# Hymba block with hierarchical MoE on one core: first weight group, gate weights and zero fills issued behind the first barrier

## The chip, the cores and the metric

One core of a Trainium2 chip runs the whole program in one launch. The metric is the device time of that core in microseconds (us). Engines are named as in the profile: PE is TensorE (matmul), PEld its weight loads, DVE is VectorE, ACT is ScalarE, POOL is GpSimd, SP is SyncE, which here only issues DMAs. A name with q behind it (SPq, POOLq, PEq) is that engine's sequencer.

## What is computed

A residual block over 4096 tokens (plus 16 meta tokens) of width 1024, then a sparse mixture of experts.

```
h = concat([meta, x])
h = h + hybrid_mixer(rmsnorm(h, mix_norm), w_in, ..., w_out)
h = h + hierarchical_moe(rmsnorm(h, ffn_norm), group_w, expert_w, w_gate, w_up, w_down)
out = rmsnorm(h, final_norm)[:, 16:]

def hybrid_mixer(u, ...):
    xb, gb, q, k, v, z, b_logit, a_logit = split(u @ w_in)     # w_in: 1024 x 3080
    y_lru = rmsnorm(rglru(xb, gb; w_r, w_i are 8 blocks of 64x64), g1)
    y_dn  = gated_deltanet(q, k, v, z, b_logit, a_logit)
    return concat([y_lru, y_dn]) @ w_out                       # w_out: 1024 x 1024
def hierarchical_moe(u, ...):
    # top-1 of 4 groups, top-2 of its 8 experts, blocks of tokens sorted by expert,
    # h = silu(x w_gate) * (x w_up);  y = h w_down;  scatter-add with the gate
```

## The kernel before

The program has four parts, each a block of five instruction streams (one for each engine) with barriers of all engines between them: an opening block (lines 320 to 410), the mixer and router (lines 478 to 1684), the experts, and the final norm. Behind the opening block stands `retire(...)` (line 412): a barrier, the clearing of semaphores by SP, and a second barrier.

In the opening block SP issues the DMAs of the first 128 tokens (`x_in`), of the router's columns (`gw`, which lies in `yl`), of the first of six groups of columns of `w_in` (`load_group(sp, "xb")`, 512 columns, 2048 KB), and, once POOL has zeroed two tiles, the four DMAs that put the blocks of `w_r` and `w_i` on the diagonals of `wr_bd` and `wi_bd`. ACT issues eight DMAs of small columns and then works out three of them, DVE zeroes state and finishes what ACT began, and POOL zeroes tiles, issues six DMAs (the last 128 rows of `u_rows` and `h_rows` in HBM from the zeroed tile `ht`, 512 KB each, and four fills of the table `idx_tab` from `qkT`, 256 KB each) and builds constants.

In the mixer's block SP issues the other five groups in the order q, k, v, gb, z, then `w_out` (4096 KB), then the second tile of x, then chunks of the experts' weights (`raw_chunks`, line 485) into `ht`, the first of which waits until the fills of the opening have landed. Each stream then runs steps i = -2, -1, 0, ... The steps -2 and -1 prepare the weights:

- DVE at i = -2: `router_columns` (L1231 to L1216), then `scale_of(0)`: L1186 takes the largest magnitude in the group xb, L1168 to L1172 with PE find it over all partitions, L1189 to L1192 make scales.
- DVE at i = -1, for each group g: `scale_of(g + 1)`, then `low_halves(g)` (L1200, eight of them). ACT makes the high halves (L887), POOL copies them into place (`high_copied`, L1692).
- The semaphore of the groups q and k is one, so `scale_of(1)` waits until both have landed.
- PE at i = -1, for g = 0 to 3: `largest` (L531, L533), `project` of group g (L578), then `router_turn` of two blocks of `w_out` (L543) and `router_through` (L553). `router_turn(0)` is the first that waits for `w_out`.
- POOL at i = -2: `level_masks` (L1706 to L1719).

From step 0 on a loop over 33 tiles of 128 tokens follows, in which PE is busy nearly all the time.

Of the kernel before, what the change touches and what calls it, by code (L numbers as in the profile page):

```python
# [21 lines left out]
P = 128  # L22
D = 1024
SEQ = 4096
# [18 lines left out]
IDX_FILLS = 2 * NE * TCAP // P // 512  # L43
# [16 lines left out]
I32 = mybir.dt.int32  # L60
# [4 lines left out]
GROUPS = ["xb", "q", "k", "v", "gb", "z"]  # L65
# [56 lines left out]
def hymba_block(nc, xm, w_in, w_out, conv_w, lru_cols, w_r, w_i, mix_g, ffn_g, final_g, dn_g, dn_a,  # L122
                dn_dt, w_router, b_router, w_gate, w_up, w_down, out):
    with ExitStack() as ctx:
        def sb(name, shape, dt=F32):
            return ctx.enter_context(nc.sbuf_tensor(name, shape, dt))
# [3 lines left out]
        def sem(name):  # L130

            if name not in sems:
                sems[name] = nc.alloc_semaphore(name=name)
            return sems[name]
# [25 lines left out]
        h_rows = nc.dram_tensor("h_rows", [SEQ + P, D], F32, kind="Internal").ap()  # L160
        u_rows = nc.dram_tensor("u_rows", [SEQ + P, D], F32, kind="Internal").ap()
        idx_tab = nc.dram_tensor("idx_tab", [NE * TCAP, 2], I32, kind="Internal").ap()
# [14 lines left out]
        wr_bd = sb("wr_bd", [P, 4, P])  # L177
        wi_bd = sb("wi_bd", [P, 4, P])
# [71 lines left out]
        qkT = sb("qkT", [P, 4, P])  # L250
# [24 lines left out]
        ht = sb("ht", [P, D])  # L275
# [38 lines left out]
        def load_group(sp, g):  # L314

            c, wide = COL[g], 512 if g != "z" else PROJ - COL["z"]
            sp.dma_start(wi[:, :, c:c + wide], w_in.rearrange("(p k) n -> p k n", k=KT)[:, :, c:c + wide]
                         ).then_inc(sem(LOADED[g][0]), 16)

        with nc.Block() as block:  # L320
            @block.sync
            def _(sp):

                sp.dma_start(x_in[:], xm[0:P, :]).then_inc(sem("x_in"), 16)
                sp.dma_start(gw, w_router.rearrange("(p k) n -> p k n", k=KT)).then_inc(sem("w_rt_in"), 16)
                load_group(sp, "xb")
                sp.wait_ge(sem("blocks_zero"), 1)

                for dst, src in ((wr_bd, w_r), (wi_bd, w_i)):
                    pair = src.rearrange("(j b) c d -> b c j d", b=2)  # L330
                    for b in range(2):
                        sp.dma_start(dst[64 * b:64 * b + 64, :, 64 * b:64 * b + 64], pair[b]).then_inc(sem("bd_in"), 16)

            @block.scalar
            def _(act):
# [41 lines left out]
            @block.gpsimd  # L377
            def _(pool):
                nc.gpsimd.memset(wr_bd[:], 0.0)
                nc.gpsimd.memset(wi_bd[:], 0.0).then_inc(sem("blocks_zero"), 1)  # L380
                nc.gpsimd.iota(io_i[:], pattern=[[1, NE]], base=0, channel_multiplier=0).then_inc(sem("iota_i"), 1)
                nc.gpsimd.iota(ip_i[:], pattern=[[0, 1]], base=0, channel_multiplier=1).then_inc(sem("iota_i"), 1)

                fill = qkT[:].rearrange("p a b -> p (a b)").bitcast(I32)
                nc.gpsimd.memset(ht[:], 0.0)
                nc.gpsimd.memset(fill, 0).then_inc(sem("zero_i"), 1)
                pool.wait_ge(sem("zero_i"), 1)
                nc.gpsimd.iota(fill.rearrange("p (m n c) -> p m n c", n=P, c=2)[:, :, :, 0], pattern=[[0, 2], [1, P]], base=SEQ,
                               channel_multiplier=0).then_inc(sem("zero_i"), 1)
                nc.gpsimd.memset(ones[:], 1.0).then_inc(sem("p_const"), 1)  # L390
                pool.wait_ge(sem("zero_i"), 2)
                for rest in (u_rows, h_rows):
                    pool.dma_start(rest[SEQ:SEQ + P, :], ht[:]).then_inc(sem("idx_zeroed"), 16)
                for n in range(IDX_FILLS):
                    pool.dma_start(idx_tab.rearrange("(p n) o -> p (n o)", p=P)[:, 512 * n:512 * n + 512],
                                   fill).then_inc(sem("idx_zeroed"), 16)
                pool.wait_ge(sem("p_const"), 1)

                nc.gpsimd.affine_select(out=ident[:], in_=ones[:], compare_op=ALU.is_equal, fill=0.0, base=0,
                                        pattern=[[1, P]], channel_multiplier=-1).then_inc(sem("p_const"), 1)  # L400
                nc.gpsimd.affine_select(out=tri[:], in_=ones[:], compare_op=ALU.is_ge, fill=0.0, base=0,
                                        pattern=[[1, P]], channel_multiplier=-1).then_inc(sem("p_const"), 1)
                nc.gpsimd.affine_select(out=kd[:, 3, :], in_=ones[:], compare_op=ALU.is_gt, fill=0.0, base=0,
                                        pattern=[[1, P]], channel_multiplier=-1).then_inc(sem("p_const"), 1)


                pool.wait_ge(sem("p_const"), 4)
                nc.gpsimd.tensor_copy(tri16[:], kd[:, 3, :]).then_inc(sem("p_const"), 1)
                nc.gpsimd.tensor_copy(ones16[:], ones[:]).then_inc(sem("p_const"), 1)
                pool.wait_ge(sem("p_const"), 6)  # L410
# [12 lines left out]
        def flat(t):  # L423
            return t[:].rearrange("p a b -> p (a b)")
# [53 lines left out]
        with nc.Block() as block:  # L478
            @block.sync
            def _(sp):  # L480
                for g in GROUPS[1:]:
                    load_group(sp, g)
                sp.dma_start(wo, w_out.rearrange("(k p) n -> p k n", p=P)).then_inc(sem("w_out_in"), 16)

                def raw_chunks(s):

                    if isinstance(s.i, int) and s.i == -1:
                        sp.wait_ge(sem("idx_zeroed"), ZEROED)
                    for n in s.sums:
                        for c in range(KT):  # L490
                            if c > 1 or n:
                                need(sp, sem("w_sq"), s.squares + KT * n + c - 1)
                            src = (w_gate, w_up)[c // 4][bass.ds(s.first + n, 1)].rearrange("o (p k) f -> p (o k f)", k=KT)
                            sp.dma_start(ht[:, 512 * (c % 2):512 * (c % 2) + 512], src[:, 512 * (c % 4):512 * (c % 4) + 512]
                                         ).then_inc(sem(f"w_raw{c % 2}"), 16)
# [1191 lines left out]
            def _(pool):  # L1687
# [36 lines left out]
                def o_copied(s, pieces):  # L1724

                    if isinstance(s.i, int) and s.i in pieces:
                        for n in range(*pieces[s.i]):
                            k, half = divmod(n, 2)
                            pool.wait_ge(sem("o_low"), n + 1)
                            nc.gpsimd.tensor_copy(wo16[:, k, w_half(True, 512 * half, 512)], o_room(n)).then_inc(sem("o_split"), 1)  # L1730

                def body(s):
                    if s.i == -2:
                        level_masks()
                    if s.i == -1:
                        for g in range(len(GROUPS)):
                            high_copied(g)
# [20 lines left out]
                    if s.G:  # L1758
                        need(pool, sem("ib_step"), 2 * s.nG)
                        need(pool, sem("gx_ready"), s.nG)  # L1760
                        b = nc.gpsimd.tensor_tensor(gx[:], gx[:], hh, ALU.mult)
                        if isinstance(s.i, int) and s.i == 0:
# [3 lines left out]
                            b = nc.gpsimd.memset(gx[:, :, 0:PAD], 0.0)  # L1766
# [415 lines left out]
```

## Time and profile before

| | |
|---|---|
| median of 3 runs | 3272.18 us |
| lowest, highest | 3269.68, 3272.93 us |
| the profiled execution's own time | 3265.26 us |
| its span, first to last instruction | 3263.7 us |
| busy: PE, DVE, ACT, POOL | 2990.4, 2590.6, 1997.9, 949.3 us |
| DMA bytes, mean rate | 380.30 MB, 117 GB/s |

The times of the views are counted from the start of the span. A row of the timeline reads: start, time taken (of all in the row), engine, line, operation, tile written <- tiles read, count, and in brackets how long the engine was idle before it and what ended that. SP's DMA rows give the time of issuing; the time to landing (the semaphore's last step) stands in the DMA views.

### The profile page before, as it was taken

The numbers are of one execution on the slowest core, as the hardware profiler recorded it, in microseconds if no ns is written. First come the engines' busy times: TensorE is split into PE (matmuls) and PEld (weight loads), VectorE is DVE, ScalarE is ACT, GpSimd is POOL, SyncE is SP. The second block draws the span as 40 slices with busy tenths as digits, with TensorE's granted clock in tenths as the row PEclk, the third lists the DMA queues.
The fourth block names the chain that finished last, engine by engine and source line by source line (L and its number), as shares of the span: only waits on it lengthen the run. The fifth ranks groups of instructions, "written<-read, shape, count | busy, mean of one in ns | idle before, by whom it ended". The sixth has DMA issues, their size and how long they took to land. (4 is left out here: it accounts for less than half of the span.)

```text
span 3263.7 us, 81939 instructions
## 1 busy us (share of the span) xinstructions
PE 2990.4 (92%) x28778; PEld 2233.3 (68%) x28779; DVE 2590.6 (79%) x7206; ACT 1997.9 (61%) x4412; POOL 949.3 (29%) x994
## 2 busy tenths in 40 slices
PE   3777999999999999999999999997699999999970
PEld 3766878888887888788878888885344555555430
DVE  6878778887887888788878887886788888888755
ACT  4555566666665656565666666653577777777646
POOL 4313122212221222132222212221344444544420
PEclk9889999999999999999999999998899999999985
DMA  7010111211212111212111111214387877677749
GB/s 264 27 53 14 47 66 65 67 66 66 72 63 76 60 67 66 73 60 73 66 66 65 68 66 66 72 56 200 118 255 222 243 202 214 187 219 216 220 99 394
DMA packets 117811, 380.30 MB, mean 117 GB/s; under 512 B 18560, under 2 KB 18688, under 8 KB 105216
## 3 DMA queue, kind: packets, MB, share of 16 engines
q1 hardware_dynamic: 82528, 269.96, 22.6%
q0 software_dynamic: 29216, 89.30, 11.9%
q10 hardware_dynamic: 5760, 16.85, 1.3%
q8 instruction: 204, 3.34, 0.4%
q14 instruction: 103, 0.84, 0.1%
HBM read 280.05 MB, written 96.01 MB: 115 GB/s over the span
## 5 line engine op out<-in xcount | busy, mean ns | idle before, releaser
L578 PE MATMUL pj<-uT,W 128*128 128x128 f16 x15840 | 982.9, 220 | 0.0
L578 PEld LDWEIGHTS pj<-uT,W 128*128 128x128 f16 x15840 | 936.8, 98 | 45.7 <-issue 37.6
L2038 DVE SCALAR_TENSOR_TENSOR W<-W,ecol 128x512 f16<-128x512 f16 x664 | 447.6, 747 | 111.9 <-ACT W L1982 107.4
L1982 ACT ACTIVATE W<-W,ecol 128x512 f16 x664 | 416.2, 710 | 79.7 <-issue 77.2
L1946 PE MATMUL bA<-W,uT 128*128 128x512 f16 x1992 | 446.6, 381 | 5.4 <-issue 4.1
L1946 PEld LDWEIGHTS bA<-W,uT 128*128 128x128 f16 x1992 | 193.5, 98 | 228.6 <-issue 9.1
L1741 POOL TENSOR_TENSOR dec<-tri,g 128x512 f32<-128x512 f32 x33 | 34.4, 1042 | 925.6 <-DVE g L1461 925.6
L1930 PE MATMUL pj<-W,qs 128*128 x664 | 301.8, 598 | 1.9 <-issue 1.0
L917 ACT ACTIVATE ht<-ht 128x512 f32<-128x512 f32 x256 | 159.9, 627 | 94.6 <-DMA ht<-w_up 90.2
L1930 PEld LDWEIGHTS pj<-W,qs 128*128 128x128 f32 x664 | 120.9, 192 | 123.3 <-issue 122.9
L947 ACT ACTIVATE qh<-bA 128x256 f32<-128x256 f32 x198 | 76.8, 388 | 193.4 <-PE bA L678 188.1
L638 PE MATMUL bO<-W,yl 128*128 128x512 f16 x768 | 186.4, 383 | 5.0 <-DVE yl L1375 5.0
L595 PE MATMUL pj<-W,uT 128*128 128x512 f16 x792 | 186.7, 379 | 0.5 <-POOL W L1692 0.5
L1777 POOL TENSOR_TENSOR yg<-aahh,gg 128x512 f32<-128x512 f32 x33 | 41.9, 1271 | 482.1 <-DVE yl L1375 457.8
L638 PE MATMUL bO<-W,yt 128*128 128x512 f16 x768 | 178.4, 378 | 0.0
L1155 DVE SCALAR_TENSOR_TENSOR qs<-ext_q,cvw,qs 128x128 f32<-128x128 f32 x396 | 168.2, 485 | 1.2
L678 PE MATMUL bA<-dec,Mt 128*128 128x128 f32 x792 | 134.2, 292 | 11.5 <-DVE dec L1303 11.1
L1906 POOL DMA_INDIRECT h_rows<-lath,sid x42 | 71.7, 1706 | 245.0 <-issue 121.1
L1906 POOL DMA_INDIRECT h_rows<-aahh,sid x41 | 71.0, 1731 | 203.6 <-issue 99.8
L595 PEld LDWEIGHTS pj<-W,uT 128*128 128x128 f16 x792 | 73.9, 98 | 71.7 <-issue 0.7
L1313 DVE COPY_PREDICATED X<-lvl,bB 128x256 f32<-128x256 uint8 x165 | 82.3, 499 | 50.5 <-PE bB L691 47.6
L691 PE MATMUL bB<-X,qh 128*128 128x128 f32 x660 | 113.4, 295 | 6.7 <-ACT qh L947 3.2
(444 smaller groups left out, 6310.0 us busy)
## 6 DMA issues: line engine op xcount, KB each, us to landing
ht<-w_gate SPq DMA_DIRECT2D x128, 256.0 KB, 3.2
ht<-w_up SPq DMA_DIRECT2D x128, 256.0 KB, 3.4
W<-w_gate SPq DMA_DIRECT2D x32, 1024.0 KB
W<-w_up SPq DMA_DIRECT2D x32, 1024.0 KB
W<-w_down SPq DMA_DIRECT2D x32, 1024.0 KB
x_in<-xm SPq DMA_DIRECT2D x33, 512.0 KB, 4.5
ht<-xm SPq DMA_DIRECT2D x32, 512.0 KB, 3.5
h_rows<-ht SPq DMA_DIRECT2D x32, 512.0 KB
```

Of the source, the lines that this page charges most:

```text
L578: mm = pe.matmul(pj[g % 2][:, j, :], w16[:, k, w_half(w_high, COL[GROUPS[g]], 512, j * P, P)], (ul if low_u else uh)[:, k, :], start=(k == ...
L595: mm = pe.matmul(flat(pj[1]), u[:, k, :], w16[:, k, w_half(w_high, c, 512)], start=(k == 0 and n_pass == 0), stop=(k == KT - 1 and n_pass ...
L638: mm = pe.matmul(bOf[:, 512 * half:512 * half + 512], y, wo16[:, j, w_half(w_high, 512 * half, 512)], start=(j == 0 and not w_high), stop= ...
L678: mm = pe.matmul(bA[:, q, :], Mt[:, 2 + q, :], crossed(T, b, P * q, HALF // b), start=True, stop=True)
L691: mm = pe.matmul(bB[:, q, :], Y[:, q, :], crossed(X, b, P * q, HALF // b), start=True, stop=True)
L917: nc.scalar.activation(ht[:, 512 * (c % 2):512 * (c % 2) + 512], ht[:, 512 * (c % 2):512 * (c % 2) + 512], ACT.Square, accum_out=sqc[:, n, ...
L1155: a = nc.vector.scalar_tensor_tensor(out=dst[:, j, :], in0=src, scalar=w, in1=dst[:, j, :], op0=ALU.mult, op1=ALU.add)
L1906: pool.indirect_dma_start(out=h_rows, out_offset=bass.IndirectOffsetOnAxis(ap=sid[par][:], axis=0), in_=yo[par], in_offset=None, compute_o ...
L1930: mm = pe.matmul(flat(pj[half]), hm2[:, j, :], w[:, j, 512 * half:512 * half + 512], start=(j == 0), stop=(j == 1))
L1946: mm = pe.matmul(flat(bA), x[:, k, :], wx[par][:, part, k, :], start=(k == 0 and part == 0 and x is uh), stop=(k == KT - 1 and x is ul))
L1982: nc.scalar.activation(part_of(wx[par][:, 0], k), raw[:, k], ACT.Copy, scale=ecol[par][:, k:k + 1]).then_inc(sem("wx_high"), 1)
L2038: a = nc.vector.scalar_tensor_tensor(out=part_of(wx[par][:, 1], k), in0=raw[:, k], scalar=ecol[par][:, k:k + 1], in1=part_of(wx[par][:, 0] ...
```

## The change

SP's opening stream keeps only the DMAs of `x_in` and the router columns. The group xb becomes the first of six in the mixer's block, and the four DMAs of `w_r` and `w_i` stand behind `w_out`, without the wait for POOL's zeroing, which the barrier now covers. POOL's six DMAs leave the opening block and stand in the mixer's block behind `level_masks`, ahead of the first `high_copied`.

```diff
             def _(sp):
                 sp.dma_start(x_in[:], xm[0:P, :]).then_inc(sem("x_in"), 16)
                 sp.dma_start(gw, w_router.rearrange("(p k) n -> p k n", k=KT)).then_inc(sem("w_rt_in"), 16)
-                load_group(sp, "xb")
-                sp.wait_ge(sem("blocks_zero"), 1)
-
-                for dst, src in ((wr_bd, w_r), (wi_bd, w_i)):
-                    pair = src.rearrange("(j b) c d -> b c j d", b=2)
-                    for b in range(2):
-                        sp.dma_start(dst[64 * b:64 * b + 64, :, 64 * b:64 * b + 64], pair[b]).then_inc(sem("bd_in"), 16)
...
                 pool.wait_ge(sem("zero_i"), 2)
-                for rest in (u_rows, h_rows):
-                    pool.dma_start(rest[SEQ:SEQ + P, :], ht[:]).then_inc(sem("idx_zeroed"), 16)
-                for n in range(IDX_FILLS):
-                    pool.dma_start(idx_tab.rearrange("(p n) o -> p (n o)", p=P)[:, 512 * n:512 * n + 512],
-                                   fill).then_inc(sem("idx_zeroed"), 16)
                 pool.wait_ge(sem("p_const"), 1)
...
-                for g in GROUPS[1:]:
+                for g in GROUPS:
                     load_group(sp, g)
                 sp.dma_start(wo, w_out.rearrange("(k p) n -> p k n", p=P)).then_inc(sem("w_out_in"), 16)
+                for dst, src in ((wr_bd, w_r), (wi_bd, w_i)):
+                    pair = src.rearrange("(j b) c d -> b c j d", b=2)
+                    for b in range(2):
+                        sp.dma_start(dst[64 * b:64 * b + 64, :, 64 * b:64 * b + 64], pair[b]).then_inc(sem("bd_in"), 16)
...
+                def table_filled():
+
+                    fill = flat(qkT).bitcast(I32)
+                    for rest in (u_rows, h_rows):
+                        pool.dma_start(rest[SEQ:SEQ + P, :], ht[:]).then_inc(sem("idx_zeroed"), 16)
+                    for n in range(IDX_FILLS):
+                        pool.dma_start(idx_tab.rearrange("(p n) o -> p (n o)", p=P)[:, 512 * n:512 * n + 512],
+                                       fill).then_inc(sem("idx_zeroed"), 16)
+
                 def body(s):
                     if s.i == -2:
                         level_masks()
+                        table_filled()
```

What stands on SP before, from the start of the opening block to the first chunks of expert weights (`yl` is the tile that holds the router columns, L153 the clearing of semaphores between the two barriers):

```order
2 L324 DMA x_in<-xm 128x1024
3 L325 DMA yl<-w_router 128x288
4 L317 DMA W<-w_in 128x8x512
5 L332 DMA wr_bd<-w_r 64x4x64 x2
6 L332 DMA wi_bd<-w_i 64x4x64 x2
7 L320 UNCONDITIONAL_BRANCH
8 L153 ISA x2
9 L479 UNCONDITIONAL_BRANCH
10 L317 DMA W<-w_in 128x8x512 x4
11 L317 DMA W<-w_in 128x8x520
12 L483 DMA W<-w_out 128x8x1024
13 L500 DMA x_in<-xm 128x1024
```

And with the change:

```order
2 L324 DMA x_in<-xm 128x1024
3 L325 DMA yl<-w_router 128x288
4 L320 UNCONDITIONAL_BRANCH
5 L153 ISA x2
6 L467 UNCONDITIONAL_BRANCH
7 L317 DMA W<-w_in 128x8x512 x5
8 L317 DMA W<-w_in 128x8x520
9 L471 DMA W<-w_out 128x8x1024
10 L475 DMA wr_bd<-w_r 64x4x64 x2
11 L475 DMA wi_bd<-w_i 64x4x64 x2
12 L492 DMA x_in<-xm 128x1024
13 L486 DMA ht<-w_gate 128x512 x4
```

The fifth 2048 KB load of `w_in` now stands in the same row of six as the others, all behind the barrier, and the small blocks stand between `w_out` and the second tile of x.

On POOL, the end of the opening block before:

```order
14 L390 MEMSET ones 128x128
15 L393 DMA u_rows<-ht 128x1024
16 L393 DMA h_rows<-ht 128x1024
17 L395 DMA idx_tab<-qkT 128x512 x4
18 L399 AFFINE_SELECT ident<-ones 128x128
19 L401 AFFINE_SELECT tri<-ones 128x128
20 L403 AFFINE_SELECT kd<-ones 128x128
```

And with the change, the place behind the masks in the mixer's block:

```order
47 L1728 DMA h_rows<-ht 128x1024
48 L1730 DMA idx_tab<-qkT 128x512 x4
49 L1684 COPY W<-rnq 128x512
50 L1684 COPY W<-decb 128x512
51 L1684 COPY W<-qh 128x512
```

The six fills (the one of `u_rows` stands in the row ahead of these) now come between the last mask and the first copy of a high half.

## Rows read from the trace of the kernel before

**Rows 1.** The page: span, and busy time of PE.

```profile
span 3263.7 us, 81939 instructions
...
PE 2990.4 (92%) x28778; PEld 2233.3 (68%) x28779; DVE 2590.6 (79%) x7206; ACT 1997.9 (61%) x4412; POOL 949.3 (29%) x994
```

**Rows 2.** Waits in 0 to 60 us (total, times, longest), then SP's queue.

```profile
POOL Mt L1706 <- POOLq L154: 9.5, 1, 9.5
...
SPq L320 <- PEq L320: 6.8, 1, 6.8
```

**Rows 3.** Timeline of the opening block and the barrier.

```profile
1.89 0.66 SPq L317 DMA_DIRECT2D W<-w_in  x1
...
3.34 0.76 ACTq L339 DMA_DIRECT2D dnc<-dn_g  x1
...
4.33 0.75 POOL L393 DMA_DIRECT2D u_rows<-ht  x1 [0.18 <-issue]
...
9.67 0.15 DVE L374 CAST tokf<-ip_i 128x1 f32<-128x1 int32 x1
...
18.69 16.57 SPq L317 DMA_DIRECT2D W<-w_in  x5
```

**Rows 4.** The four idx_tab fills: issue time, starts, time to landing.

```profile
L395 POOL DMA_DIRECT2D idx_tab<-qkT x4: 542/544/547, 5.6 to 7.2; - x4
...
DMA to landing us min/median/max: 9.0/9.7/10.2
```

**Rows 5.** Issues, KB each, us to landing: before 18.6 us, then at 18.69.

```profile
W<-w_in SPq DMA_DIRECT2D x1, 2048.0 KB, 15.7
...
dnc<-dn_g ACTq DMA_DIRECT2D x1, 0.5 KB, 9.1
...
W<-w_in SPq DMA_DIRECT2D x1, 2048.0 KB, 9.2
```

**Rows 6.** Timeline of DVE behind the barrier.

```profile
18.73 0.73 DVE L1231 TENSOR_TENSOR yl<-yl,fg 128x288 f32<-128x288 f32 x1 [8.92 <-PEq L154]
...
23.77 4.42 DVE L1186 TENSOR_REDUCE wmx<-W 128x8 f32<-128x4096 f32 x1
...
32.37 0.21 DVE L1445 TENSOR_SCALAR rxc<-xst,rdsc 128x1 f32<-128x1 f32 x1
33.02 4.42 DVE L1186 TENSOR_REDUCE wmx<-W 128x8 f32<-128x4096 f32 x1 [0.45 <-DMA W<-w_in]
```

**Rows 7.** Timeline where w_out is first used.

```profile
59.73 0.53 PEld L543 LDWEIGHTS bA<-ident,W 128*128 128x128 f32 x4 [0.17 <-DMA W<-w_out]
...
66.04 0.28 DVE L1170 TENSOR_REDUCE wm<-bO 1x1 f32<-1x128 f32 x1 [2.60 <-PE bO L531]
```

**Rows 8.** Busy time by stretch; last: PEclk, DMA share, GB/s.

```profile
18.00:20.50 2.50, 0.37 (x1) 0.08 (x1) 1.26 (x3) 1.79 (x2) 1.64 (x3) 1.00 0.11 12
...
24.00:32.00 8.00, 2.05 (x9) 1.27 (x7) 6.62 (x11) 1.93 (x4) 6.60 (x20) 1.00 1.05 399
```

**Rows 9.** Timeline of POOL: first mask, last mask, first copy.

```profile
18.71 0.72 POOL L1706 TENSOR_SCALAR_AFFINE_SELECT Mt<-ones 128x128 f32<-128x128 f32 x1 [9.52 <-POOLq L154]
...
31.16 0.53 POOL L1719 CAST lvl<-ot 128x128 uint8<-128x128 f32 x2
46.09 0.62 POOL L1692 COPY W<-rnq 128x512 f16<-128x512 f16 x1 [14.40 <-DVE W L1200]
```

**Rows 10.** DMA queues (packets, MB, share) in 7 to 8 us, then 8 to 16 us.

```profile
q1 hardware_dynamic: 183, 0.37, 96.1%
...
q0 software_dynamic: 560, 1.97, 60.3%
q1 hardware_dynamic: 631, 1.25, 40.1%
```

**Rows 11.** Timeline: first use of an expert chunk, of wr_bd.

```profile
76.88 0.65 ACT L917 ACTIVATE ht<-ht 128x512 f32<-128x512 f32 x1
...
125.27 0.97 PEld L785 LDWEIGHTS bC<-xc,wr_bd 128*128 128x128 f32 x8
```

More of the change, by code:

```diff
@@ L379, in _ @@
                 nc.gpsimd.memset(wr_bd[:], 0.0)
-                nc.gpsimd.memset(wi_bd[:], 0.0).then_inc(sem("blocks_zero"), 1)
+                nc.gpsimd.memset(wi_bd[:], 0.0)
                 nc.gpsimd.iota(io_i[:], pattern=[[1, NE]], base=0, channel_multiplier=0).then_inc(sem("iota_i"), 1)
```

## The prediction

> **What bounds the kernel now.** I read the page first: PE is busy 92% of a span of 3263.7 us [rows 1], and everything that the change touches lies in the first 130 us, ahead of the loop in which PE is full. So a shift of the start of that loop passes to the end one for one, and the question is only where the loop starts. Next the waits and the timeline of the opening. DVE's last work there starts at 9.67 and takes 0.15, so all compute is done at 9.82; the first instruction behind the barrier is SP's at 18.69 [rows 3]. The reader is to see a hole of 8.9 us: POOL is idle 9.5 us and SP's queue stands 6.8 us at the block's end [rows 2]. What ends then? POOL's last fill was issued at 7.2 and took 10.2 us to land, 17.4 [rows 4]; xb, issued at 1.89, took 15.7, 17.6 [rows 3, 5]. Either could hold the barrier; POOL's own idling speaks for the fills (POOL seems to leave the block only when its DMAs have landed). Both leave the opening in the changed kernel, so I needn't choose.
>
> Behind the barrier I followed DVE and asked which wait ends last. The router's columns take 18.73 to 23.77, then xb's reduction starts at once: xb had landed. After scales and two casts DVE is free at 32.58 (32.37 and 0.21) and starts on q at 33.02, 0.45 of it a wait for the DMA of q and k [rows 6]. So up to there DVE and the loads run level. The second place is PE's first turn of `w_out` at 59.73, with a wait of 0.17 for its DMA [rows 7]: again level. After it DVE waits 2.60 for PE at 66.04 [rows 7], so lateness of PE there isn't absorbed. In 24 to 32 us the DMA engines show a share of 1.05 and 399 GB/s [rows 8]: **the loads are limited by rate**, and the opening is a race between the DVE chain and a full DMA system.
>
> **The change, step by step.**
>
> *The barrier opens earlier.* It needs POOL (free earlier, since its issues go), ACT and DVE. DVE ends at 9.82. From the landing of the last fill to SP's first issue were 17.4 to 18.69, 1.25 us, which holds both barriers and the clearing. So SP issues at 9.8 + 1.25 = 11.1 at the latest by this chain; ACT's and DVE's few us may shrink a little without the other DMAs. I take 10.8 (10.3 to 11.1). That is 7.9 earlier than 18.69. An upper bound: if the block's end also waits for the small columns, the last of them (issued 3.34, 9.1 to land under the old load, 12.4 [rows 3, 5]) gives 12.4 + 1.25 = 13.7.
>
> *xb.* The first load behind the barrier took 9.2 us to land [rows 5], so xb lands at 10.8 + 9.2 = 20.0. DVE's router work (23.77 − 18.73 = 5.0) ends at 15.8, so a new wait of about 4 us stands ahead of xb's reduction, which then starts at 20.0 in place of 23.77: 3.8 of the 7.9 are left.
>
> *q and k.* DVE wants them 32.58 − 23.77 = 8.8 later, at 28.8. Before they landed 33.02 − 18.69 = 14.3 behind the first issue. Now xb, 2048 KB (2.10 MB), is ahead: at 399 GB/s 5.26 us. So 10.8 + 14.3 + 5.3 = 30.4, without the fills. With them: POOL's masks last 13.0 (18.71 to 31.69, the last row's 31.16 and 0.53 [rows 9]), so the fills are issued from 23.8. Before, the first was issued at 4.33 [rows 3] and its queue (q0) carries nothing in 7 to 8 us but 1.97 MB in 8 to 16 [rows 10]; so data flow some 3.7 us after issue, at 27.5. Then q0 had 60% of the engines and q1 (SP's) 40%. At 27.5 the load of k lacks 2.9 us of full rate, which at 40% are 7.2: it lands at 34.7. DVE starts on q at 34.7, against 33.02: **+1.7**. Bounds: 30.4 (−2.6) if the fills come too late to matter, 35.7 (+2.7) if all of them go ahead.
>
> The Trainium skill, "DMA: Bandwidth & Descriptors", section "Queues, rings and completion order", says that a DMA engine takes turns between the rows it has work for, a packet at a time. By equal turns in bytes k would land at 27.5 + 5.8 = 33.3, +0.3; the trace's 60 to 40 in bytes decides here.
>
> *w_out, which decides.* Before, from SP's first issue to PE's start on it: 59.73 − 18.69 = 41.0, all at full rate. Now the same, plus xb, plus the fills (2 × 512 + 4 × 256 = 2048 KB, so again 5.26): 10.8 + 41.0 + 5.3 + 5.3 = **62.4**. PE would be ready at 59.56 + 1.7 = 61.3, so it waits about 1 us for `w_out`, and `router_turn(0)` starts 2.6 later than before. The same from the other side: the DMA engines had moved some 5 MB by 18 us (0.5 of x, 2.1 of xb, 2.1 of fills, 0.4 of small ones), then stood almost idle (12 GB/s in 18 to 20.5 [rows 8]); now they stand idle from about 6 to 13 us, and idle DMA time is what costs.
>
> *From there on* everything is a chain of DVE, PE and ACT of unchanged length. DVE's own part is 1.7 late and PE's 2.6, so DVE's wait of 2.60 for PE grows and the 2.6 goes through.
>
> *Costed at nothing:* POOL's six issues (4.33 to 7.8, 3.5 us) move from an opening that POOL left at 9.2 (18.71 less 9.52 idle) into its idle 14.4 us before the first copy at 46.09 [rows 9]; they would cost only if they took over 14 us. The blocks of `w_r`, `w_i`: 256 KB behind `w_out`, 0.7 us at full rate and, since the pieces are small, up to a few times that, say 3; first used at 125.27 [rows 11], so 55 us of cover. The second tile of x and the first expert chunks, queued on SP behind them, (1 MB, 2.6 us) land near 62.4 + 3 + 2.6 = 68 in place of 59.7 + 2.6 = 62.3; ACT takes the first chunk at 76.88 [rows 11], cover 9 us. SP's added issues lie in a queue that only waits for room.
>
> **Sum.** +2.6 us. The profiled execution would read 3265.3 + 2.6 = 3267.9, and the median of the runs shown, which lies 6.9 above the profiled execution, 3272.2 + 2.6 = 3274.8. That is 0.08%; 0.2% (6.5 us) is about what a measurement of this kernel can tell from no change.
>
> **The rivals.**
>
> *A. The fills don't delay the loads* (they come late, or their writes go beside the reads). Then `w_out` lands at 57.1, k at 30.4, and PE's start is ruled by both: −2.6, 3269.6. For it: nothing in the rows but that fills write and loads read. Against: 1.97 and 1.25 MB in 8 to 16 add up to the same 400 GB/s [rows 10]. Half of this gives 0.
>
> *B. The barrier opens late,* at 13.7, held by the small columns: 2.9 more, +5.5, 3277.7. Against: the small columns should land sooner without xb and the fills beside them.
>
> *C. The whole gain of the barrier comes through:* −7.9, 3264.3, faster by 0.24%. It needs loads that aren't limited by rate; the share of 1.05 speaks against it.
>
> *D. Slower: POOL is held up in issuing the fills.* Its copies of xb's high halves (from 46.09) gate PE's first projection. The issues start at 23.8 and have until about 48; each took about 0.55 us in the opening, when DVE was nearly idle. Above 4 us each they push that copy late; at 6 us each POOL is free at 59.8, 13.7 later than 46.09: 3286. Against: then DVE runs the one long reduction of xb, and beside that same reduction POOL worked unhindered (6.60 us busy in 24 to 32, DVE 6.62 [rows 8]).
> The Trainium skill, "SBUF — State Buffer", in its warning on DVE blocking DMA, states that a DMA issued from GpSimd takes about 3.1 us in place of 0.62 beside a VectorE copy that holds the shared port. By that figure six would take 18.6 us, an estimate from that page alone, and end at 42.4, still in time; no run here shows it yet.
>
> **Chances.** Forecast (between +1 and +4, 3273 to 3276.5) 0.60; A with its halves 0.17; B 0.12; C 0.04; D 0.04; and 0.03 for what I don't see. Faster by over 0.2%: C and a little more, 0.06. Slower by over 0.2%: D, B's upper end and the scatter of builds, 0.10. Within: 0.84. The range reaches down past A (3269.6) and up past B (3277.7), with 1 us for the scatter of medians (3269.7 to 3272.9 among the runs): 3268.5 to 3279.
>
> **What would show it.** SP's first issue behind the barrier at 10.8; a DVE wait of some 4 us for `W<-w_in` ahead of xb's reduction at 20; a second of some 6 us ahead of q's at 34.7; PE's first L543 (now about eight lines higher) at 62.3 with a wait for `w_out`; fills issued at 23.8 and landed near 36; from there every stage 2.6 later. Wrong would be: a first issue near 18, k landed at 30, or PE ready well after `w_out`.

## The result and the profile after

| | before | after |
|---|---|---|
| median | 3270.1 us (20 runs) | 3274.92 us (20 runs) |
| lowest, highest | 3262.92, 3278.24 us | 3264.2, 3287.09 us |
| the profiled execution's own time | 3265.26 us | 3277.19 us |

Run beside each other, the changed kernel takes 1.0018 times as long, with an interval of 1.001 to 1.0026: 5.9 us more (3.3 to 8.5). I had forecast 2.6 us more, and a time of 3274.8 us. That the time fits is luck. The shift itself is about twice what I said, and in the trace nearly three times; what makes up for it is that the median that I had added it to, 3272.2 of 3 runs, lies 2.1 us above the median of 20.

The timeline at the barrier, in the changed kernel (a row reads: start, time, engine, line, operation, tiles, count, idle time before and what ended it):

```profile
8.81 0.14 DVE L367 CAST tokf<-ip_i 128x1 f32<-128x1 int32 x1
10.14 17.76 SPq L317 DMA_DIRECT2D W<-w_in  x5
10.16 0.72 POOL L1698 TENSOR_SCALAR_AFFINE_SELECT Mt<-ones 128x128 f32<-128x128 f32 x1 [4.46 <-POOLq L154]
...
19.05 4.42 DVE L1178 TENSOR_REDUCE wmx<-W 128x8 f32<-128x4096 f32 x1 [3.87 <-DMA W<-w_in]
...
23.46 0.76 POOL L1728 DMA_DIRECT2D u_rows<-ht  x1 [0.32 <-POOL lvl L1711]
32.01 4.42 DVE L1178 TENSOR_REDUCE wmx<-W 128x8 f32<-128x4096 f32 x1 [4.17 <-DMA W<-w_in]
```

The barrier opens at 10.14 in place of 18.69 [rows 3]. The hole of 8.9 us is gone, and two new ones stand in DVE: 3.87 us for xb and 4.17 us for q and k. DVE reaches q at 32.01, 1.0 us earlier than before [rows 6]. So of 8.55 us won at the barrier, 1.0 is left 22 us later. This second wait differs between executions: experiment 3 below, whose instructions are the same up to there, has it at 6.13 us and DVE on q at 33.94.

The same timeline where `w_out` is first used, with the first and last of PE's work on it and the row of DVE that waits for it:

```profile
63.15 0.71 PE L535 MATMUL bA<-ident,W 128*128 128x128 f32 x4 [3.60 <-DMA W<-w_out]
...
65.16 1.06 PE L535 MATMUL bT<-ident,W 128*128 128x128 f32 x4
...
70.99 1.90 PE L545 MATMUL bO<-yl,zs 128*128 128x36 f32 x8
...
73.14 0.28 DVE L1162 TENSOR_REDUCE wm<-bO 1x1 f32<-1x128 f32 x1 [10.80 <-PE bO L523]
```

PE waits 3.60 us for `w_out` and starts on it 3.42 us later than before (63.15 against 59.73 [rows 7]). But DVE's next row starts at 73.14 against 66.04 [rows 7], 7.10 later. Between the two rows lie the same turns and products, in 9.99 us where they took 6.31. Nothing was added there. The table by stretches tells why. Its columns are: stretch, length, busy time and instructions of PE, PEld, DVE, ACT and POOL, the granted share of TensorE's clock, the DMA share and GB/s. In the changed kernel:

```profile
54.00:59.50 5.50, 5.50 (x72) 5.37 (x70) 5.50 (x7) 3.17 (x6) 1.89 (x4) 1.00 1.02 407
59.50:63.00 3.50, 0.04 (x1) 0.00 (x0) 2.77 (x3) 0.69 (x1) 2.63 (x5) 1.00 1.15 260
63.00:64.50 1.50, 1.35 (x9) 1.35 (x10) 0.00 (x0) 0.00 (x0) 0.00 (x0) 0.82 0.99 305
...
66.00:69.00 3.00, 3.00 (x17) 3.00 (x15) 0.00 (x0) 1.08 (x2) 0.00 (x0) 0.50 0.01 4
69.00:72.70 3.70, 3.70 (x20) 3.70 (x19) 0.00 (x0) 0.00 (x0) 0.00 (x0) 0.50 0.00 0
72.70:77.60 4.90, 4.35 (x37) 3.99 (x38) 3.61 (x10) 2.48 (x5) 0.00 (x0) 0.50 0.00 0
77.60:82.00 4.40, 4.40 (x74) 4.40 (x72) 4.40 (x9) 3.17 (x6) 1.43 (x3) 1.00 0.02 4
```

And in the kernel before, where PE goes from the projection into the turns without a hole:

```profile
62.00:65.70 3.70, 3.54 (x32) 3.57 (x33) 1.37 (x3) 1.00 (x3) 1.23 (x3) 1.00 0.00 0
```

PE stands still from 59.55 to 63.15. About 1 us after it takes up work again, its granted clock falls from 1.00 (2.4 GHz) to 0.50 (1.2 GHz) and stays there up to 77.6: a turn takes 1.06 us in place of 0.61, the last product 1.90 in place of 1.06 (each full-speed value is seen again in an experiment below). The wait costs twice: once as a wait, 3.4 us, and once in the clock, 3.7 us. Not all of the low stretch is new. In the kernel before, PE's clock also falls, at 66.6 behind a wait of 0.55 us, and comes back at 70.0:

```profile
66.60:69.90 3.30, 3.30 (x29) 3.29 (x30) 2.59 (x7) 1.88 (x4) 0.00 (x0) 0.50 0.00 0
```

There it meets the second projection, which takes 6.90 us in all, and 7.16 in the changed kernel. The 3.7 us are lost in the turns and products ahead of it.

The end of the setup, by the yardstick of [rows 11]:

```profile
132.62 0.97 PEld L777 LDWEIGHTS bC<-xc,wr_bd 128*128 128x128 f32 x8
```

132.62 against 125.27 is +7.35. Two more differences of this one execution lie behind it. In 250 to 262 us the clock is 0.86 in the mean, where before it was 1.00 (first the changed kernel, then the one before). The traces of all eight experiments have such a dip too, between 241 and 261 us, so here it is the one trace of the kernel before that stands apart:

```profile
250.00:262.00 12.00, 9.93 (x113) 9.66 (x111) 11.35 (x23) 6.05 (x16) 5.78 (x7) 0.86 0.00 1
```

```profile
250.00:262.00 12.00, 9.96 (x146) 9.55 (x145) 11.83 (x25) 7.34 (x16) 6.83 (x8) 1.00 0.01 1
```

The experts' stage shows the rest, in the list of groups by line (least, median and most ns of one, first and last start), changed kernel and kernel before:

```profile
L1948 PE MATMUL bA<-W,uT x1992: 376/379/634, 2328.6 to 3166.0; 128*128 128x512 f16 x200
```

```profile
L1946 PE MATMUL bA<-W,uT x1992: 376/379/634, 2319.8 to 3154.5; 128*128 128x512 f16 x200
```

It begins 8.8 us later and its last product starts 11.5 us later. The 7.35 of the setup are well explained. Of the 4 us more, 1.5 arise between the setup and this stage and 2.7 in it; with them the profiled pair differs by 11.9, twice the 5.9 of the timed ratio. The same instructions run in this stage in all ten kernels profiled, and it takes 829 to 844 us from the first to the last start (834.7 before, 837.4 with the change). I take the 2.7 for scatter; that is argued, not tested.

### The profile page after: what moved, and what is told of

It is laid out like the page before. It is cut to its first block and busy times, and to the rows that moved or that the text cites. A ratio compares the mean times of both kernels' runs of the same rounds, so it can differ in the third digit from the quotient of the medians.

```text
span 3275.6 us, 81939 instructions
## 1 busy us (share of the span) xinstructions
PE 2998.3 (92%) x28778; PEld 2239.9 (68%) x28779; DVE 2590.4 (79%) x7206; ACT 1998.0 (61%) x4412; POOL 947.4 (29%) x994
## 3 DMA queue, kind: packets, MB, share of 16 engines
q0 software_dynamic: 29216, 89.30, 11.9%
## 5 line engine op out<-in xcount | busy, mean ns | idle before, releaser
L1948 PEld LDWEIGHTS bA<-W,uT 128*128 128x128 f16 x1992 | 194.0, 98 | 229.3 <-issue 10.3
L670 PE MATMUL bA<-dec,Mt 128*128 128x128 f32 x792 | 134.5, 293 | 11.1 <-DVE dec L1295 10.6
```

The costliest lines, as they stand in the source:

```text
L670: mm = pe.matmul(bA[:, q, :], Mt[:, 2 + q, :], crossed(T, b, P * q, HALF // b), start=True, stop=True)
L1948: mm = pe.matmul(flat(bA), x[:, k, :], wx[par][:, part, k, :], start=(k == 0 and part == 0 and x is uh), stop=(k == KT - 1 and x is ul))
```

## The experiments

"Yardstick" is the start of the first use of `wr_bd`, 125.27 before and 132.62 with the change. It is read from one profile of each kernel, and the ratio from all its timed runs. The next column is a second mark some 11 us further on, PE's first transpose of `x_in` in step 0, at 136.62 before; why it is needed is shown in experiment 6. Experiments 5 to 8 ran on another chip than 1 to 4. Their ratios compare with the kernel before on the same chip, their yardsticks with its one profile on the first. How far the yardstick scatters isn't known: with the same instructions ahead of it, the landing of k differs by 1.9 us between the change and experiment 3, and that of `w_out` by 0.3.

| kernel | yardstick | against before | second mark against before | ratio of times (interval) |
|---|---|---|---|---|
| the change | 132.62 | +7.35 | +7.09 | 1.0018 (1.001 to 1.0026) |
| 1 fills late | 123.12 | −2.15 | −2.23 | 0.9991 (0.9981 to 1.0001) |
| 2 xb early | 124.73 | −0.54 | +1.25 | 1.0006 (0.9992 to 1.002) |
| 3 PE filled | 128.59 | +3.32 | +3.59 | 1.0004 (0.9992 to 1.0015) |
| 4 blocks early | 128.94 | +3.67 | +5.44 | 1.0016 (1.0003 to 1.0028) |
| 5 xb early, fills late | 118.51 | −6.76 | −7.09 | 0.997 (0.9958 to 0.9982) |
| 6 xb and q early, fills late | 117.57 | −7.70 | −5.27 | 0.998 (0.9969 to 0.9991) |
| 7 before, only xb moved | 128.25 | +2.98 | +3.26 | 1.0011 (0.9998 to 1.0025) |
| 8 before, w_out late | 133.80 | +8.53 | +9.32 | 1.0013 (1.0001 to 1.0024) |

**My theory** has two parts. (a) The fills, now in the middle of the weight loads, and xb, now behind the barrier, push `w_out` back more than the barrier's 8.55 us give. (b) PE's wait for it lowers the clock, and that costs as much again. **Rivals**: the fills don't delay the loads (the prediction's A); the clock falls for another reason than PE's wait; the small blocks behind `w_out` have no part.

### 1. The fills behind the second copy of POOL

```diff
                     if s.i == -2:
                         level_masks()
-                        table_filled()
                     if s.i == -1:
...
                             high_copied(g)
+                            if g == 1:
+                                table_filled()
```

> The changed kernel, with POOL's six fills issued behind the second group's high copies (near 54 us) instead of behind the masks (near 24 us); nothing else. Theory (the fills' 2.1 MB go ahead of the weights, w_out is late, and PE's clock falls while it waits): k lands at 10.1 + 14.3 + 5.3 = 29.7 in place of 32.0, w_out at 10.1 + 41.0 + 5.3 = 56.5, up to 57.8 with the small blocks behind it, in place of 63.1; PE is ready near 56.3 and waits under 1.5 us, so the turns of w_out run at full clock. Step 0 starts 2 to 3 us earlier than before the change, where the changed kernel starts it 7.1 later: 9 to 10 us faster than the changed kernel. Rival (the fills don't delay the loads, lateness comes from xb alone): w_out still lands near 62 to 63 and the start stays some 7 later than before.

The timeline of this kernel:

```profile
30.06 4.42 DVE L1178 TENSOR_REDUCE wmx<-W 128x8 f32<-128x4096 f32 x1 [2.23 <-DMA W<-w_in]
...
57.60 0.71 PE L535 MATMUL bA<-ident,W 128*128 128x128 f32 x4 [0.42 <-DMA W<-w_out]
58.15 0.61 PE L535 MATMUL bB<-ident,W 128*128 128x128 f32 x4
...
62.70 1.06 PE L545 MATMUL bO<-yl,zs 128*128 128x36 f32 x8
```

Without the fills `w_out` is there at 57.60 and not at 63.10: 5.5 us, which is their 2048 KB at 400 GB/s (5.3 us). k is there 1.95 us sooner. PE waits only 0.42 us, keeps its full clock, and turns and products take 6 us. The yardstick is 9.5 us earlier than with the change. The ratio, 0.9991, isn't clear of 1. Rival A is refuted: here the fills, which write to HBM, and the loads, which read from it, share one rate. (POOL issued the fills from 60.16, later than the 54 that I had expected, and so behind all of `w_out`.)

### 2. xb back in the opening

```diff
                 sp.dma_start(gw, w_router...
+                load_group(sp, "xb")
...
-                for g in GROUPS:
+                for g in GROUPS[1:]:
                     load_group(sp, g)
```

> The changed kernel, with the first weight group xb issued again in the opening block; the fills stay behind the masks and the small blocks behind w_out. Theory: the barrier still opens near 10.1 (the fills held it, not xb), DVE runs 8.6 us ahead of before up to the end of the second group; w_out lands at 10.1 + 41.0 + 5.3 (fills) = 56.4, up to 57.8. PE is ready near 51 and waits 5 us or more, its clock falls to the lower level, and the turns take 9.5 us in place of 6.0: step 0 starts at about +1 against before. Without the clock part it would be -2.6. Rival (xb's DMA held the barrier too): SP's first issue behind it comes only once xb has landed, at 11 to 12 us or later.

The timeline, and from the DMA view the issue of xb (KB, us to landing), which was made at 1.89:

```profile
10.72 1.27 SPq L317 DMA_DIRECT2D W<-w_in  x2
...
57.76 1.12 PE L536 MATMUL bA<-ident,W 128*128 128x128 f32 x4 [5.80 <-DMA W<-w_out]
```

```profile
W<-w_in SPq DMA_DIRECT2D x1, 2048.0 KB, 10.4
```

xb landed at 12.3, and the barrier had opened at 10.72. So it isn't xb, loaded by SP, that held the barrier before. `w_out` lands 5.4 us sooner than with the change, about what xb's 2048 KB are worth, and yet PE waits longer, 5.80 us, since it was ready sooner as well. The clock is low again, but from the first turn on: that row takes 1.12 us where experiment 1 shows 0.71. It had fallen during the wait, at 55.7, and is back at 62.5, in the middle of the products. So turns and products took 7.6 us and not the 9.5 that I had expected; the longest wait of all has a small second price. The yardstick, −0.54, is earlier than my "about +1"; the second mark, at +1.25, is where I had put it.

### 3. Work for PE in place of the wait

The changed kernel, with 22 transposes of constants that nothing reads, put between the first projection and the first turn. The kernel does this work in addition.

```diff
+                            if g == 0:
+                                pe.wait_ge(sem("uT_ready"), 1)
+                                for k in range(22):
+                                    pe.transpose(bC[:, k % 4, :], ones[:], ident[:])
                             router_turn(2 * g)
```

> The changed kernel, with 22 more transposes on PE (ones by the identity into a bank that is free then; nobody reads them) between the first projection and the first turn of w_out, so that PE is busy for most of the 3.6 us in which it waited. Theory (the clock fell because PE stood idle): w_out still lands at 63.1, the turns and products behind it take 6.0 us as before the change and not 9.5, and step 0 starts 3.4 to 3.7 later than before the change and not 7.1. Rival (the turns are slow for another reason, such as small DMA packets or late reads of W): they still take 9.5 us and the start stays at +7.1.

The timeline of PE, and the stretches of this kernel:

```profile
60.17 2.57 PE L702 MATMUL bC<-ident,ones 128*128 128x128 f32 x22
62.84 0.71 PE L535 MATMUL bA<-ident,W 128*128 128x128 f32 x4
...
67.94 1.06 PE L545 MATMUL bO<-yl,zs 128*128 128x36 f32 x8
```

```profile
60.00:62.80 2.80, 2.74 (x28) 2.50 (x25) 2.80 (x1) 0.69 (x1) 2.80 (x6) 1.00 1.19 240
62.80:69.00 6.20, 5.79 (x49) 5.52 (x49) 1.36 (x3) 2.06 (x4) 1.22 (x3) 1.00 0.40 124
```

The first turn starts at 62.84, as late as in the changed kernel (63.15), but the clock stays at 1.00 and the last product starts at 67.94 and not at 70.99. The gain is 3.05 − 0.31 = 2.7 us by the start of that row, 0.84 more by its length, 3.6 in all; the yardstick gains 4.0. The ratio moves the same way, though its interval overlaps that of the change. The experiment isn't quite clean. Its code differs only in the added work, but in this execution k landed at 33.92 in place of 31.99:

```profile
33.94 4.42 DVE L1182 TENSOR_REDUCE wmx<-W 128x8 f32<-128x4096 f32 x1 [6.13 <-DMA W<-w_in]
```

So PE's projection ended at 60.33 and not at 59.55, and the wait that the added work filled would have been about 2.5 us, not 3.6. Part (b), that the wait itself costs the clock, rests on this experiment together with 7 and 8: in 7 PE starts on `w_out` as late as here with no wait and no fall, in 8 a wait of 2.88 us brings the fall into the kernel before.

### 4. The blocks of w_r and w_i back in the opening

```diff
+                sp.wait_ge(sem("blocks_zero"), 1)
+                for dst, src in ((wr_bd, w_r), (wi_bd, w_i)):
+                    ... (the four DMAs, as before the change)
...
                 sp.dma_start(wo, w_out...
-                for dst, src in ((wr_bd, w_r), (wi_bd, w_i)):
-                    ...
```

POOL's second zeroing also signals `blocks_zero` again, as before the change.

> The changed kernel, with the four DMAs of w_r and w_i issued in the opening block behind x and the router columns (with the wait for POOL's zeroing) instead of behind w_out. Theory (the 1024 small packets queued behind w_out slow its tail by 1.3 us: the loads took 53.0 us from the first issue in place of 51.6 by bytes): w_out lands at about 61.8, PE waits 2.3 us. Step 0 then starts at +2.1 if the clock holds, at +5.7 if it falls all the same. Rival (the 1.3 us are the general pace of the loads): w_out lands at 63.1 and everything stays at +7.1. The barrier stays near 10.1 in both.

The DMA view of 60 to 62 us, when the tail of `w_out` is under way, first in the changed kernel and then in this one:

```profile
DMA packets 853, 0.47 MB, mean 233 GB/s; under 512 B 785, under 2 KB 785, under 8 KB 853
```

```profile
DMA packets 222, 0.80 MB, mean 399 GB/s; under 512 B 20, under 2 KB 20, under 8 KB 221
```

In the changed kernel 785 of 853 packets are under 512 bytes: they are the small rows of `w_r` and `w_i`, served in turn with the last rows of `w_out`, and the rate is down to 233 GB/s at full engines. They were issued behind `w_out`, and yet 48 of the 64 steps of their semaphore had come by 62.81, ahead of the last of `w_out` at 63.10. Without them `w_out` landed 51.7 us after SP's first issue, against 53.0 (63.10 − 10.14) in the change and 52.7 in experiment 3. The sum by bytes gives 51.6. So I had costed at nothing what took 1.0 to 1.3 us. It landed at 62.47 and not at the 61.8 that I had expected, because the barrier opened at 10.81, 0.7 us later than with the change; DVE's last work in the opening ended that much later. The timeline shows what else it gave:

```profile
62.52 0.71 PE L537 MATMUL bA<-ident,W 128*128 128x128 f32 x4 [2.91 <-DMA W<-w_out]
```

A wait of 2.91 us still pulls the clock down, from 63.3 to 66.7 only, and turns and products take 7.0 us. The yardstick: +3.67, between the two values that I had named for a clock that holds (+2.1) and one that falls (+5.7).

### 5. and 6. A version that is faster than both

Experiment 5 joins 1 and 2: xb stays in the opening, the fills go behind the second copy. Experiment 6 also takes q into the opening, and keeps its semaphore over the barrier.

```diff
                 sp.dma_start(gw, w_router...
+                load_group(sp, "xb")
+                load_group(sp, "q")          # experiment 6 alone
...
-                for g in GROUPS:
+                for g in GROUPS[1:]:         # experiment 6: GROUPS[2:]
                     load_group(sp, g)
```

> The changed kernel with both: xb issued in the opening, and POOL's fills issued behind the second group's high copies; the small blocks stay behind w_out. Theory (only DMA bytes ahead of k and w_out, and PE's idle wait, cost time): SP's first issue behind the barrier at 10.7, k lands at 10.7 + 14.3 = 25.0, w_out at 10.7 + 41.0 = 51.7, up to 53 with the small blocks' tail; PE is ready near 51.8 and waits 0 to 1.3 us, no fall of its clock. Step 0 starts 7 to 8 us earlier than before the change, about 0.2% of the whole. Rival (something else in the changed opening costs, such as the blocks or the new order on POOL): less than 4 us earlier.

> As the kernel before it, and with the second group q too issued in the opening. Theory: barrier near 10.7 again although q then still has some 5 us to load (hardware-issued loads don't hold it), the DMA engines never stand idle, w_out lands near 47 to 48, PE waits for nothing: step 0 starts 8 us earlier than before the change. Rival 1 (xb's landing did hold the barrier, and in the kernel with xb early it only happened to be over in time): SP's first issue behind the barrier is near 16. Rival 2 (the loads are no longer what binds): the same start as with xb alone early, so that q early gives under 1 us.

The timeline of experiment 5:

```profile
10.75 10.91 SPq L317 DMA_DIRECT2D W<-w_in  x4
...
25.01 4.42 DVE L1179 TENSOR_REDUCE wmx<-W 128x8 f32<-128x4096 f32 x1 [0.43 <-DMA W<-w_in]
...
52.89 0.71 PE L536 MATMUL bA<-ident,W 128*128 128x128 f32 x4 [0.42 <-DMA W<-w_out]
```

Both new waits of DVE are gone (0.43 is left of them), PE meets `w_out` with 0.42 us of wait, 6.84 us earlier than the kernel before, and the yardstick passes it on: −6.76. The measured ratio, 0.997, is 9.8 us (5.9 to 13.7). It has the lowest ratio of this study, though its interval overlaps that of experiment 6, and the shift of the start accounts for it within its interval. It and the change were not timed beside each other; each was timed beside the kernel before.

Experiment 6 has DVE wait for no DMA at all on q (24.61), and PE start on `w_out` at 51.77 with no wait. Its q landed at 18.05, and the barrier opened at 10.86. Of the 1.1 us that it leads, 0.94 reach the yardstick and none shows in the total (0.998, against 0.997). Behind the yardstick, at 117.57, the clock is at half speed, where experiment 5 has 1.00 (first 6, then 5):

```profile
120.90:127.70 6.80, 6.12 (x18) 3.32 (x19) 6.52 (x17) 4.59 (x11) 3.87 (x5) 0.50 0.01 2
```

```profile
121.00:128.00 7.00, 5.41 (x28) 2.94 (x29) 6.86 (x15) 5.21 (x12) 4.92 (x7) 1.00 0.01 2
```

The same projection runs there in both (again first 6, then 5):

```profile
123.44 7.47 PE L589 MATMUL pj<-W,uT 128*128 128x512 f16 x24
```

```profile
123.75 5.34 PE L588 MATMUL pj<-W,uT 128*128 128x512 f16 x24 [0.75 <-POOL W L1685]
```

It takes 2.1 us longer, and the work behind it, the second mark of the table, starts at 131.35 in experiment 6 and at 129.53 in experiment 5: the lead has become a lag of 1.8 us. A like dip, 3.4 us long, stands behind the yardstick in experiments 2, 3, 4, 7 and 8 and not in the kernel before, the change, 1 and 5. Why it comes in some and not in others wasn't tested; PE's wait ahead of it is 2.84 us in experiment 6 and 2.87 in the change, which has no dip.

I had expected `w_out` at 47 to 48 in experiment 6. It landed at 51.0, only 1.8 us earlier than in experiment 5 (52.85). The bytes are the same, so issuing q early can win only the time in which the engines weren't full. From 11 to 16 us they moved 1.27 MB in experiment 5 and 1.95 MB in experiment 6, and the difference is 1.7 us at 400 GB/s. There was no hole of 5.3 us left to fill.

### 7. The kernel before, with xb alone moved

```diff
-                load_group(sp, "xb")
                 sp.wait_ge(sem("blocks_zero"), 1)
...
-                for g in GROUPS[1:]:
+                for g in GROUPS:
```

> The kernel before, with xb's load alone moved behind the barrier; the fills and the small blocks stay in the opening. Theory (POOL's fills hold the barrier, and idle DMA time is what makes w_out late): the fills land at 8.2 + 5.3 = 13.5 now that they have the engines to themselves, SP's first issue at 13.5 + 1.25 = 14.8, k lands at 14.8 + 14.3 + 5.3 = 34.4, w_out at 14.8 + 41.0 + 5.3 = 61.1; PE is ready at 61.0 and hardly waits, so its clock holds: step 0 starts 1.4 later than before. Rival (the barrier isn't held by the fills): it opens at 10.1 to 11.2 and w_out lands at 57.5.

The four `idx_tab` fills were issued up to 7.2, as before. Their landing by the DMA view, and the barrier by the timeline:

```profile
DMA to landing us min/median/max: 5.9/6.6/7.7
```

```profile
16.20 0.58 SPq L317 DMA_DIRECT2D W<-w_in  x1
16.22 0.72 POOL L1705 TENSOR_SCALAR_AFFINE_SELECT Mt<-ones 128x128 f32<-128x128 f32 x1 [7.03 <-POOLq L154]
```

The last fill landed at 14.96, and 1.24 us later the barrier opened. Before it was 17.45 and 18.69. With xb gone from the opening, the barrier still stands 7 us behind all compute; with the fills gone (experiment 2) it doesn't, though xb is still under way. So the fills held it. I had expected them to land at 13.5, but the DMA engines moved only 253 GB/s in 8 to 14 us, with the fills nearly alone on them. The other surprise: `w_out` came late, at 62.57, and PE started on it at 62.61 with no wait, since PE was as late itself (q's reduction starts at 35.80, 2.8 later than before). The clock stayed at 1.00 through turns and products, and the yardstick is +2.98 (I had said +1.4), as late as the start on `w_out`. Late without waiting costs once.

### 8. The kernel before, with w_out alone late

1.5 MB of input rows are loaded ahead of `w_out` into tiles that aren't in use yet; nothing reads them. They share the semaphore of `w_out`, so PE and DVE now wait for all five loads, and DVE also ahead of the low halves of the group k; `w_out` had long landed by then.

```diff
                     load_group(sp, g)
+                for n, (t, c) in enumerate(((lath, D), (aahh, D), (ks, 512), (vs, 512))):
+                    sp.dma_start(flat(t), xm[P * n:P * n + P, 0:c]).then_inc(sem("w_out_in"), 16)
                 sp.dma_start(wo, w_out...
```

> The kernel before, with 1.5 MB more loaded by SP ahead of w_out (rows of x into four tiles that are free then; nobody reads them), which makes w_out 3.9 us late and nothing else. Theory (a wait of PE of about 4 us also lowers its clock): PE's first turn starts near 63.6, the turns and products take about 9.5 us in place of 6.0, step 0 starts 7 to 7.5 later than before, as in the changed kernel. Rival (the slow turns in the changed kernel come from its own order of things): they take 6.0 and step 0 starts 3.9 later.

The stretches of this kernel:

```profile
61.50:64.00 2.50, 0.00 (x0) 0.00 (x0) 2.43 (x3) 0.52 (x1) 2.43 (x5) 1.00 1.02 398
65.70:69.00 3.30, 3.30 (x17) 2.96 (x15) 0.00 (x0) 1.84 (x4) 0.00 (x0) 0.50 0.02 6
69.00:73.40 4.40, 4.40 (x22) 4.40 (x22) 0.00 (x0) 0.00 (x0) 0.00 (x0) 0.50 0.00 0
```

With nothing of the change in it, the wait of 2.88 us ahead of the first turn (64.17) brings the same fall to 0.50, from 65.6 to 79.3. Turns and products take 9.25 us (9.54 in the change, 6.0 in experiment 1). The yardstick is +8.53: 4.4 are the later start (64.17 against 59.73), 3.3 the slow turns and products, and 0.7 the projection behind them, 7.62 us in place of 6.90. This experiment, 7 and 3 together show that the fall in the turns and products comes with PE's wait ahead of them and goes with it. They don't show how long it lasts once it has come.

## Why the prediction was right and wrong

**The barrier**, "So SP issues at 9.8 + 1.25 = 11.1 at the latest ... I take 10.8": right, 10.14, a little below my lower end (10.3), because DVE's last work ended 0.9 us earlier, at 8.95. "Either could hold the barrier": experiments 2, 6 and 7 show that it was the fills. Rival B (13.7) didn't come.

**xb**, "lands at 20.0 ... a new wait of about 4 us": right; DVE starts on it at 19.05, after 3.87 us.

**q and k**, "it lands at 34.7 ... +1.7": in the change 31.99 and −1.0, and 33.92 and +0.9 in experiment 3, with the same instructions up to there. The share was right: in 28 to 34 us the fills had 66% of the engines and the loads 39%. I had said that k would lack 2.9 us of full rate when the fills' data begin. Without the fills it landed at 30.04 (experiment 1), 2.2 us behind 27.8, when their data began. In experiment 3 the loads had 38.3% of the engines from 27.8 to its landing, 2.3 us of full rate, as this says; in the change 36.5% of 4.2 us, only 1.5. So the sum holds for experiment 3 but for the earlier barrier, and why k landed 1.9 us sooner in the profiled change stays open. In the change, in 28 to 34 us (packets, MB, share of the engines):

```profile
q0 software_dynamic: 450, 1.58, 66.0%
...
q1 hardware_dynamic: 449, 0.89, 38.7%
```

450 packets against 449: turn and turn about, and who has the longer packets gets the more bytes. The Trainium skill, "DMA: Bandwidth & Descriptors", "Queues, rings and completion order", says that an engine takes turns a packet at a time. The equal counts agree with it. My sentence "By equal turns in bytes" misread the rule; in packets it and the trace give the same.

**w_out**, "10.8 + 41.0 + 5.3 + 5.3 = 62.4": this sum held to 0.75 us (63.15): −0.66 from the barrier and +1.0 to +1.3 from the small blocks, which I had "costed at nothing" by counting only the 55 us until someone needs them, and not that they are served in turn with the load ahead of them. Experiments 1 and 2 confirm the two terms of 5.3 singly (5.5 and 5.4).

**PE's wait**, "it waits about 1 us": it was 3.60. Of the 2.5 us more, 0.75 is the later `w_out`; the greater part, 1.75, is that DVE was 1.0 early where I had it 1.7 late, so PE was ready at 59.55, not at 61.3. With k as in experiment 3 PE was ready at 60.33 and would have waited about 2.5 us. The forecast start on `w_out` hardly depends on this, and so it looked harmless.

**"From there on everything is a chain of DVE, PE and ACT of unchanged length"**: this is the step that failed, and with it the size. PE's part of the chain depends on its clock. Behind 3.6 us of idling the clock was at 0.50 from 64.0 to 77.6, and the turns and products took 3.7 us more. Experiment 3 took this away (3.6 us), experiment 7 was as late without it, and experiment 8 made it in the kernel before (3.3 us). The Trainium skill, "TensorE: Matmul & The Clock Gate", Part 1, describes the gate and its two levels; the trace agrees in the levels, 1.00 and 0.50. By that page, a forecast of a wait on PE should have carried a second price, and mine didn't name it even as a rival.

**The rivals.** A is refuted by experiment 1. C is refuted: of 8.55 us nothing came through. D didn't come: POOL's six issues took 23.46 to 26.93, at 0.54 to 0.76 us each. But they did not meet what D feared. DVE's reduction of xb ended as they began, at 23.47, and beside them ran only DVE's small work; how long a POOL issue takes beside a long reduction, no run here shows.

**The chances.** The result, +5.9 (3.3 to 8.5), lies on the edge of what I called "within 0.2%" (6.5 us). As a shift, the forecast of +1 to +4 missed the middle of it; as a time, 3273 to 3276.5, it holds the median, by the luck named above. "Slower" deserved more than 0.10.

Open: the 4 us behind the setup in the profiled pair; the landing of k; why the low clock lasts 3.4 us behind one wait and 13.7 behind another; and why PE's first projection took 8.34 us (from 51.21) in the changed kernel and 7.43 (from 52.30) before, both at full clock, so that PE was ready for `w_out` no earlier than before although DVE led by 1.0 us.

## What to carry to other kernels

Where the DMA engines are full from the first load to the last, work out when the last load lands, from the bytes and from the time in which the engines stand idle; an earlier barrier is worth only as much as it lets the loads start sooner, and loads that can be issued ahead of it should be. Bytes that nobody waits for belong behind the loads on which the chain hangs, and many small packets well behind them: queued right behind a load they still delayed it by about 1 us here. And a wait on PE has two prices, the wait and the clock behind it: compare the waits of PE, not only the start times, and make what feeds it early or PE busy.

## What I had not expected of the hardware

- After an idle wait of 3.60 us PE's granted clock fell to 0.50 about 1 us after work had begun again, and stayed there 13.7 us though PE was busy for most of them. After 2.91 us (experiment 4) it stayed low 3.4 us, after 2.88 us (experiment 8) 13.7 us. In the wait of 5.80 us (experiment 2) it fell before the wait was over and stayed low 6.8 us. Equal waits, unequal prices: 1.0 us to 3.7 us for the same work, and 1.6 us for the longest wait.
- The barrier opened 1.25 us behind the landing of POOL's own last DMA (17.45 and 18.69 before, 14.96 and 16.20 in experiment 7, 17.59 and 18.84 in experiment 8), long after POOL's last instruction. DMAs that SP issued don't hold it: xb landed 1.6 us and q 7.2 us behind the opened barrier.
- 785 packets under 512 bytes in 2 us took the engines from 399 to 233 GB/s, though the load ahead of them had been issued 3.6 us or more before them, and most of them landed ahead of its last row.
- The data of POOL's first fill began 4.3 us behind its issue in the change (23.46 to about 27.8), where SP's loads kept the DMA engines full, and about 1.3 us behind it in experiment 1 (60.16 to about 61.4), where the engines stood idle.
